# A transformer kernel on one core: two norm reductions placed later, an early strip split, halves in attention, and splits done one stage ahead

## The chip, the cores and the metric

The kernel runs on one core of one Trainium2 chip, in a single launch. The metric is device time in microseconds (us), the median of three runs. The engines are TensorE (PE, the matrix unit), VectorE (DVE), ScalarE (ACT), GpSimd (POOL) and SyncE (SP, which only issues transfers here).

## The reference

Two blocks run one behind the other on 512 tokens of width 1024 (256 context tokens beside them in the first block), all in float32:

```python
# first block, two layers
ax = modulate(rmsnorm(h, norm1_g[l]), mx[0], mx[1])
yx, yc = mixing_layer(ax @ w_in[l], ac @ w_in[l], ...)      # pooling, neighbourhood attention, retention
h = h + mx[2] * (yx @ w_out[l])                             # output projection
h = h + mx[5] * conv_ffn(modulate(rmsnorm(h, norm2_g[l]), mx[3], mx[4]), w_up[l], ..., w_down[l])
# conv_ffn: u = h @ w_up; a 3-tap convolution; (silu(a) * b) @ w_down, with 2816 hidden columns
# second block, one layer
h = rms(x, mix_norm_g); p = h @ w_in
a_out = mla(...)                                            # latent attention, 8 heads
h_out = hyena(...)                                          # long convolutions through DFTs
x = x + concat(rms(a_out), rms(h_out)) @ w_out
x = x + mem_xattn(rms(x), rms(mem), ...)                    # memory attention, 4 heads
x = x + hier_moe(rms(x), ...)                               # 32 experts
```

## The kernel before, in words

Activations lie transposed in SBUF: 8 tiles of 128 features by 512 or 768 columns (tokens, and the context's in the first layer). Weights come from HBM as 178 "strips" of up to 128x2048 float32, in the order in which they are used, into a ring of three slots.

**High and low parts.** TensorE takes float32 here only as a rounded form. So each operand is split in two: ScalarE writes the rounded value (`split_high`, L824), VectorE subtracts it from the value (`split_low`, L859), and three matmuls (high weight by low source, high by high, low by high) take the place of one. A strip's high part goes into one of two buffers that alternate, so the split of strip s waits until strip s-2 has been used up; its low part is written over the strip. Sources (the activation tiles) are split in the same way, each into a room of its own.

**`project` (L878 to L1028)** is one stage: it multiplies all sources by a list of strips. A unit is one output tile: it runs over all sources (`for j, tile in enumerate(u.tiles)`), six matmuls a source at 768 columns (three parts by two pieces) and three at 512. `split_order` (L908 to L923) is the order for both ScalarE and VectorE, written out by hand:

```python
if not ahead:
    split_strip(0)
following = max(1, ahead)
for k in range(tiles_ahead, len(sources)):
    if k == early and following < 2:
        split_strip(following)
        following += 1
    split_tile(k)
for i in range(len(units)):
    while following < total and (following < 2 or self.freed_at[first + following - 2] < ends[i]):
        split_strip(following)
        following += 1
    if deferred and i == 0:
        norm()
    take(i)
```

`take(i)` on VectorE evicts unit i from PSUM; on ScalarE it adds a bias or does what the stage hangs on it, once VectorE has taken unit i. `norm()` comes before `take(0)`. Strip 2 is split in turn i = 2 where strip 0 serves units 0 and 1, which is after `norm()`, `take(0)` and `take(1)`. `ahead` says that the first strip was split in the stage before, `tiles_ahead` how many sources were, and `early` ahead of which source strip 1 is split (if not given: behind all of them).

**Deferred norms.** The RMS norm in front of a projection is applied to its outputs. Beside the matmuls, ScalarE squares the tiles, VectorE adds the squares, TensorE sums them over partitions with a matmul by ones (`mean`, L437, or L533 in `PairNorm`), ScalarE takes the root, VectorE the reciprocal, and the eviction multiplies by it. TensorE does the summing matmul in `before(pe, 2)`, ahead of unit 2. `Deferred` serves the input projection of both layers (12 strips, two units each) and the up projection, `PairNorm` the second block's input projection (`second_projection`, 8 strips, two units each; its two sums and two roots make a longer chain).

**The stages around it.** A layer is input projection, pooling, neighbourhood attention, (context attention in layer 0), retention, output projection, up projection, down projection. In the down projection a unit needs two strips of 11 sources each, out of 22 sources. Layer 1's up projection splits the first 9 of these sources and the first strip ahead; layer 0's splits none. Retention splits the first strip of the output projection ahead, but no source. `attention` (L1030) runs over units of 128 queries (32 units in the latent attention, 16 in the memory attention): scores, maximum and scaling on VectorE (`top`, `normalise`), exponentials on ScalarE, transposes (L1123), a copy on ScalarE, products with the values at each head's end. Both of these attentions split the next stage's two first strips ahead: ScalarE in unit 4, VectorE in unit 5. No stage begins on any engine until all engines have left the one before.

## Time and profile before

| | |
|---|---|
| median of 3 runs | 2773.83 us (2773.24 to 2775.17) |
| the profiled execution: its own time | 2779.62 us |
| the profiled execution: span, first to last instruction | 2777.8 us |
| mean granted TensorE clock | 0.949 of full speed |
| TensorE busy | 2487.8 us (90% of the span), 14602 matmuls |
| VectorE busy | 1375.2 us (50%) |
| ScalarE busy | 868.5 us (31%) |
| GpSimd busy | 251.7 us (9%) |
| TensorE waiting, longest groups | 25.0, 24.9, 15.1, 13.8, 13.3 us |

The span is 1.8 us shorter than the execution's own time: that much lies around it. The profiled execution took 5.8 us more than the median of the runs. A wait is given with the engine and line of the instruction that ended it. A granted clock of 0.50 is TensorE at 1.2 GHz, 1.00 is 2.4 GHz.

### The profile page before, as it was taken

What the parts mean: (1) busy time and instruction counts of PE and PEld (TensorE: products, weight loads), DVE (VectorE), ACT (ScalarE), POOL (GpSimd) and SP (SyncE); (2) the same over time, 40 slices, a digit from 0 to 9 for tenths busy, and PEclk for the clock granted to TensorE, in tenths of its full rate; (3) what the DMA queues carried; (4) which work ended last, traced back from release to release, by engine and by line L of the source; (5) the groups of instructions that cost most, each with busy time, mean ns of one, the idle gap of its engine ahead of it and who ended that gap; (6) DMA issues with size and microseconds to landing.
All of it is one profiled execution on the core that took longest, in us unless ns stands there. A gap on an engine that the chain in (4) does not pass through costs nothing. (4 is left out here: it accounts for less than half of the span.)

```text
span 2777.8 us, 34833 instructions
## 1 busy us (share of the span) xinstructions
PE 2487.8 (90%) x14602; PEld 1933.5 (70%) x14602; DVE 1375.2 (50%) x2185; ACT 868.5 (31%) x1385; POOL 251.7 (9%) x183
## 2 busy tenths in 40 slices
PE   7997988999998998997889999998977889898976
PEld 5885657888887787995669998764733368573322
DVE  4324554566667214325647777347565645423213
ACT  3222433332324113223444334233424642311001
POOL 0002520000000000003500000000042020011112
PEclk9998989999999999997989999999988999988999
DMA  5114731111111112115612223320201013348997
GB/s 240 61 54 106 269 128 46 46 61 61 63 69 38 53 63 82 61 69 142 224 46 92 92 92 117 111 82 31 87 0 54 0 61 137 121 188 326 421 421 292
DMA packets 58555, 326.88 MB, mean 118 GB/s; under 512 B 8157, under 2 KB 14429, under 8 KB 26461
## 3 DMA queue, kind: packets, MB, share of 16 engines
q1 hardware_dynamic: 45358, 302.76, 29.4%
q0 software_dynamic: 5696, 12.59, 1.2%
q10 hardware_dynamic: 7344, 9.28, 1.0%
q8 instruction: 117, 1.92, 0.3%
q14 instruction: 40, 0.33, 0.0%
HBM read 317.26 MB, written 12.58 MB: 119 GB/s over the span
## 5 line engine op out<-in xcount | busy, mean ns | idle before, releaser
L953 PE MATMUL ps<-work_rounded,ring_rounded 128*128 128x512 f32 (+1 forms) x2016 | 537.0, 354 | 19.1 <-DVE work_rounded L397 10.6
L953 PE MATMUL ps<-xn_rounded,ring_rounded 128*128 128x512 f32 (+2 forms) x2304 | 541.8, 347 | 0.0
L2003 PE MATMUL ps<-xn_rounded,ring_rounded 128*128 128x258 f32 (+2 forms) x2816 | 535.1, 312 | 0.0
L2003 PEld LDWEIGHTS ps<-xn_rounded,ring_rounded 128*128 128x128 f32 x2816 | 414.6, 191 | 31.2
L953 PEld LDWEIGHTS ps<-xn_rounded,ring_rounded 128*128 128x128 f32 x2304 | 373.4, 191 | 57.6 <-issue 0.2
L953 PEld LDWEIGHTS ps<-work_rounded,ring_rounded 128*128 128x128 f32 x2016 | 336.5, 192 | 76.3 <-DVE work_rounded L397 11.8
L953 PE MATMUL ps<-big_rounded,ring_rounded 128*128 128x512 f32 (+1 forms) x1200 | 326.3, 364 | 45.0 <-DVE big_rounded L859 25.0
L859 DVE TENSOR_TENSOR ring_rounded<-ring,ring_rounded 128x2048 fp32r<-128x2048 f32 (+2 forms) x94 | 189.1, 2015 | 266.5 <-ACT ring_rounded L824 266.5
L2003 PE MATMUL ps<-work_rounded,ring_rounded 128*128 128x256 f32 (+1 forms) x1232 | 280.2, 309 | 9.0 <-PEq L784 4.8
L953 PEld LDWEIGHTS ps<-big_rounded,ring_rounded 128*128 128x128 f32 x1200 | 203.4, 196 | 84.8 <-DVE ring_rounded L859 21.4
L824 ACT ACTIVATE ring_rounded<-ring 128x2048 fp32r<-128x2048 f32 (+2 forms) x94 | 158.2, 1687 | 314.7 <-PE ps L953 298.3
L2003 PEld LDWEIGHTS ps<-work_rounded,ring_rounded 128*128 128x128 f32 x1232 | 191.9, 191 | 21.5 <-issue 10.6
L2052 DVE TENSOR_TENSOR ring_rounded<-ring,ring_rounded 128x1024 fp32r<-128x1024 f32 x84 | 103.0, 1226 | 171.4 <-ACT ring_rounded L2017 171.4
L2017 ACT ACTIVATE ring_rounded<-ring 128x1024 fp32r<-128x1024 f32 x84 | 89.0, 1060 | 205.8 <-PE ps L2003 205.8
L2022 ACT ACTIVATE work<-work,small 128x512 f32<-128x512 f32 (+1 forms) x132 | 81.5, 649 | 203.0 <-DVE work L2059 203.0
L1313 ACT ACTIVATE big<-big,small 128x512 f32<-128x512 f32 (+1 forms) x81 | 47.0, 624 | 254.0 <-DVE big L1309 154.0
L1303 DVE COPY small<-ps 128x2 f32<-128x2 f32 x46 | 7.3, 159 | 176.9 <-PE ps L953 176.6
L3320 PE MATMUL ps<-big,work 128*64 128x512 f32 x352 | 80.4, 604 | 15.1 <-DMA big<-in_experts 13.8
L1339 POOL MEMSET work<- 128x792 f32 x2 | 1.5, 758 | 1015.4 <-DMA work<-in_pool 1015.4
L2070 DVE SCALAR_TENSOR_TENSOR work<-work,vec 128x769 f32<-128x769 f32 (+1 forms) x88 | 78.0, 887 | 3.1
L2069 DVE SCALAR_TENSOR_TENSOR work<-work,vec 128x769 f32<-128x769 f32 (+1 forms) x88 | 78.0, 887 | 3.1
L3343 ACT ACTIVATE work<-ps,small 128x256 f32<-128x256 f32 x16 | 7.6, 476 | 221.3 <-PE ps L3320 221.3
(420 smaller groups left out, 3125.4 us busy)
## 6 DMA issues: line engine op xcount, KB each, us to landing
ring<-in_stream SPq DMA_DIRECT2D x141, 1024.0 KB, 4.8
big<-in_experts SPq DMA_DIRECT2D x44, 1024.0 KB, 26.0
ring<-in_stream SPq DMA_DIRECT2D x32, 704.0 KB, 4.0
ring<-in_experts SPq DMA_DIRECT2D x22, 1024.0 KB, 27.3
xn<-in_experts SPq DMA_DIRECT2D x15, 1024.0 KB, 28.4
work<-in_experts SPq DMA_DIRECT2D x15, 1024.0 KB, 28.7
big<-in_first_modulation SPq DMA_DIRECT2D x8, 1024.0 KB, 14.1
work<-in_bias ACTq DMA_DIRECT2D x24, 256.0 KB, 3.9
```

The source lines that it names most:

```text
L824: return act.activation(self.rounded(high), value, ACT.Copy)
L859: return dve.tensor_tensor(self.rounded(value), value, self.rounded(high).bitcast(F32), ALU.subtract)
L953: mm = pe.matmul(out[:, a - u.first:b - u.first], lhs, rhs, start=j == 0 and n == 0 and not u.onto, stop=j == terms - 1 and n == len(passe ...
L1313: act.activation(px[:, m, a:z], px[:, m, a:z], ACT.Identity, bias=bias[:, m, s:s + 1])
L2003: mm = pe.matmul(out[:, a:b], ws[:, k, :], x[k][:, a - base:b - base], start=k == 0 and n == 0, stop=k == KT - 1 and n == 2)
L2017: act.activation(high_w[c], half(i, c)[0], ACT.Copy).then_inc(strip_high.up(), 1)
L2022: ins = act.activation(u[:, i % 2, c, o:o + b - a], u[:, i % 2, c, o:o + b - a], ACT.Identity, bias=bias[:, i % 2, c, s:s + 1])
L2052: dve.tensor_tensor(low_part, value, high_w[c].bitcast(F32), ALU.subtract).then_inc(strip_low.up(), 1)
L2069: settle(dve, dve.scalar_tensor_tensor(out=cc, in0=uu[:, 0:n], scalar=cw(0, t), in1=cc, op0=ALU.mult, op1=ALU.add), vstep)
L2070: dve.scalar_tensor_tensor(out=cc, in0=uu[:, 2:2 + n], scalar=cw(2, t), in1=cc, op0=ALU.mult, op1=ALU.add).then_inc(convolved.up(), 1)
L3320: mm = pe.matmul(b.bank(2)[r, :], self.rows_t[:, k, r], self.gu[s][:, k, :], start=k == 0, stop=k == KT - 1)
L3343: act.activation(self.silu_t, b.bank(2)[:, 0:256], ACT.Silu, scale=b.slot_scale[:, 0, n:n + 1]).then_inc(self.silued, 1)
```

## The change

1. `PairNorm`: the two summing matmuls stand ahead of unit 4 and no longer ahead of unit 2.
2. `Deferred` in `project`: the summing matmul stands inside unit 2, after five of its eight sources, and no longer ahead of it.
3. `attention`: the two strips that are split ahead are split in four halves of 1024 columns, on ScalarE in units 4, 6, 8 and 10, on VectorE in units 5, 7, 9 and 11.
4. Down projections: strip 1 is split ahead of source 8 (layer 0) or 10 (layer 1) and no longer behind all sources.
5. Layer 0's up projection splits the down projection's first strip and first source at its end. Both retentions split the first source of the output projection.

```diff
 class PairNorm:  def before(self, pe, i):
-        if i == 2:
+        if i == 4:
             pe.wait_ge(b.sig("squares_added").sem, b.sig("squares_added").at(2 * KT - 2))
 project, tensor:
-                    if deferred:
+                    if deferred and not (i == 2 and type(deferred) is Deferred):
                         deferred.before(pe, i)
...
                         mine = j * len(u.need) // terms
+                        if i == 2 and j == 5 and type(deferred) is Deferred:
+                            deferred.before(pe, i)
 attention, vector:
+                def halves_low(part):
+                    for _, value, high in views[part // 2:part // 2 + 1]:
+                        r = slice(part % 2 * 1024, part % 2 * 1024 + value.shape[1] // 2)
+                        dve.wait_ge(strip_high.sem, strip_high.at(part + 1))
+                        self.split_low(dve, value[:, r], high[:, r])
...
-                    if u == 5:
-                        self.low_ahead(dve, views)
+                    if u in (5, 7, 9, 11):
+                        halves_low((u - 5) // 2)
 attention, scalar:
-                    if u == 4:
-                        self.high_ahead(act, views)
+                    if u in (4, 6, 8, 10):
+                        halves_high((u - 4) // 2)
 retention, scalar (behind root(0)):
+                act.wait_ge(weighed.sem, weighed.at(6))
+                for value, high in mixed:
+                    self.split_high(act, value, high).then_inc(next_high.up(), 1)
                 act.activation(self.small[:, 124:125], self.ones[:, 0:1], ACT.Ln)
                 square(2)
 retention, vector:
                 gate(2)
+                for n, (value, high) in enumerate(mixed):
+                    dve.wait_ge(next_high.sem, next_high.at(n + 1))
+                    self.split_low(dve, value, high)
                 normalise(1)
 ffn_up, scalar (layer 0 only):
+                    if (i, c) == (FT - 1, 1) and need_ctx:
+                        act.wait_ge(done.sem, done.at(2 * FT))
+                        strip_ahead(act)
                 silu(FT - 1)
+                if need_ctx:
+                    act.wait_ge(gated.sem, gated.at(len(runs)))
+                    self.split_high(act, *down_sources[0]).then_inc(next_high.up(), 1)
 ffn_up, vector (layer 0 only):
                 convolve(*halves_of[-1])
+                if need_ctx:
+                    strip_low_ahead(1)
                 gate(FT - 1)
+                if need_ctx:
+                    dve.wait_ge(next_high.sem, next_high.at(2))
+                    self.split_low(dve, *down_sources[0])
 down_sources (layer 0):
-            rooms, ahead = tiles_in(width, self.xn, self.work), 0
+            rooms, ahead = tiles_in(width, self.xn, self.work), 1
 ffn_down:
-        self.project(units, 2 * KT, finish, banks_each=2, sources=sources, tiles_ahead=tiles_ahead,
+        self.project(units, 2 * KT, finish, banks_each=2, sources=sources, tiles_ahead=tiles_ahead, early=10 if last else 8,
 layer: output_projection(...)
+                               tiles_ahead=1)
```

## Rows read from the trace of the kernel before

**Rows 1.** Waits of TensorE over the whole span: total, times, longest (us).
```profile
PE ps L953 <- DVE big_rounded L859: 25.0, 3, 12.1
PE ps L1123 <- DVE work L1156: 24.9, 21, 6.0
```

**Rows 2.** Timeline, second block's input projection, TensorE: start, length, idle before.
```profile
1920.23 1.98 PE L533 MATMUL ps<-xn,base 128*128 128x512 f32 x4 [2.30 <-DVE xn L547]
...
1937.35 0.79 PE L953 MATMUL ps<-work_rounded,ring_rounded 128*128 128x512 f32 x1 [4.02 <-DVE ring_rounded L859]
```

**Rows 3.** Timeline of the same stage, ScalarE and VectorE.
```profile
1933.06 1.91 ACT L824 ACTIVATE ring_rounded<-ring 128x2048 fp32r<-128x2048 f32 x1 [7.74 <-DVE big L2291]
...
1935.00 2.29 DVE L859 TENSOR_TENSOR ring_rounded<-ring,ring_rounded 128x2048 fp32r<-128x2048 f32 x1 [2.03 <-ACT ring_rounded L824]
```

**Rows 4.** Timeline, input projection of layer 0, TensorE and VectorE.
```profile
59.12 1.45 PE L437 MATMUL ps<-work,base 128*128 128x512 f32 x4
...
71.61 2.29 DVE L859 TENSOR_TENSOR ring_rounded<-ring,ring_rounded 128x2048 fp32r<-128x2048 f32 x1 [3.01 <-ACT ring_rounded L824]
...
77.36 0.51 PE L953 MATMUL ps<-work_rounded,ring_rounded 128*128 128x512 f32 x2
```

**Rows 5.** Timeline, input projection of layer 1, TensorE.
```profile
1109.81 2.93 PE L437 MATMUL ps<-work,base 128*128 128x512 f32 x4 [2.77 <-DVE work L412]
...
1125.14 0.47 PE L953 MATMUL ps<-work_rounded,ring_rounded 128*128 128x256 f32 x2 [0.72 <-DVE ring_rounded L859]
```

**Rows 6.** Timeline, end of layer 0's up projection and start of its down projection.
```profile
887.62 1.03 DVE L2077 TENSOR_TENSOR big<-work 128x512 f32<-128x512 f32 x2
889.01 1.38 ACT L824 ACTIVATE ring_rounded<-ring 128x1408 fp32r<-128x1408 f32 x1 [3.32 <-PEq L784]
...
891.96 7.04 DVE L859 TENSOR_TENSOR big_rounded<-big,xn_rounded 128x768 fp32r<-128x768 f32 x8
...
893.05 0.98 PE L953 MATMUL ps<-big_rounded,ring_rounded 128*128 128x512 f32 x2 [12.07 <-DVE big_rounded L859]
...
911.07 3.16 DVE L859 TENSOR_TENSOR ring_rounded<-ring,ring_rounded 128x1408 fp32r<-128x1408 f32 x2
912.74 1.01 PE L953 MATMUL ps<-big_rounded,ring_rounded 128*128 128x512 f32 x2 [5.70 <-DVE ring_rounded L859]
```

**Rows 7.** Timeline, start of layer 1's down projection, VectorE.
```profile
1733.05 1.62 DVE L859 TENSOR_TENSOR ring_rounded<-ring,ring_rounded 128x1408 fp32r<-128x1408 f32 x1
```

**Rows 8.** Timeline, retention's end and output projection's start, both layers.
```profile
418.57 0.84 ACT L1779 ACTIVATE big<-big 128x768 f32<-128x768 f32 x1 [0.51 <-DVE big L1870]
...
427.18 5.98 ACT L824 ACTIVATE work_rounded<-big 128x768 fp32r<-128x768 f32 x8 [1.56 <-PEq L784]
429.07 1.01 PE L953 MATMUL ps<-big_rounded,ring_rounded 128*128 128x512 f32 x2 [7.18 <-DVE big_rounded L859]
...
1409.34 4.27 ACT L824 ACTIVATE work_rounded<-big 128x512 fp32r<-128x512 f32 x8 [1.24 <-PEq L784]
1410.74 0.80 PE L953 MATMUL ps<-big_rounded,ring_rounded 128*128 128x512 f32 x1 [5.74 <-DVE big_rounded L859]
```

**Rows 9.** Attention's strip splits (timeline), and half-size splits (the page's groups).
```profile
2162.37 4.50 DVE L859 TENSOR_TENSOR ring_rounded<-ring,ring_rounded 128x2048 fp32r<-128x2048 f32 x2 [1.35 <-ACT ring_rounded L824]
...
2406.42 0.69 PE L1123 MATMUL ps<-base,work 128*128 128x128 f32 x2 [5.68 <-DVE work L1156]
...
L2052 DVE TENSOR_TENSOR ring_rounded<-ring,ring_rounded 128x1024 fp32r<-128x1024 f32 x84 | 103.0, 1226 | 171.4 <-ACT ring_rounded L2017 171.4
L2017 ACT ACTIVATE ring_rounded<-ring 128x1024 fp32r<-128x1024 f32 x84 | 89.0, 1060 | 205.8 <-PE ps L2003 205.8
```

**Rows 10.** Windows behind three waits: us, busy by engine, then the granted clock.
```profile
912.70:917.00 4.30, 4.26 (x13) 3.68 (x14) 1.53 (x1) 0.00 (x0) 0.00 (x0) 0.50 0.00 0
1109.80:1112.60 2.80, 2.79 (x5) 1.57 (x6) 0.00 (x0) 0.00 (x0) 0.00 (x0) 0.50 0.48 202
...
1937.30:1942.60 5.30, 5.25 (x13) 4.15 (x14) 3.27 (x3) 1.91 (x1) 0.00 (x0) 0.52 0.03 14
```

More of the change, by code:

```diff
@@ L1058, in attention @@
         views = self.split_ahead(ahead)
-        next_high = self.sig("next_high")
+        next_high, strip_high = self.sig("next_high"), self.sig("strip_high")
+        assert all(value.shape[1] == STRIP for _, value, _ in views)
         def pair_at(u, place):
@@ L1197, in exponentials, with halves_high @@
                                    accum_out=stat[:, 2, b:b + 1]).then_inc(exped.up(), 1)
+                def halves_high(part):
+                    for n, value, high in views[part // 2:part // 2 + 1]:
+                        r = slice(part % 2 * 1024, part % 2 * 1024 + value.shape[1] // 2)
+                        self.strip(act, n)
+                        self.split_high(act, value[:, r], high[:, r]).then_inc(strip_high.up(), 1)
                 def square_pair(p):
@@ L1654, in retention @@
         half = [slice(0, 64), slice(64, 128)]
+        next_high = self.sig("next_high")
+        mixed = [(px[:, MIXED[k], 0:qw], w[:, k * qw:(k + 1) * qw]) for k in range(1)]
         def update(c, d, p):
@@ L1979, in views @@
         def views():
-            return self.split_ahead(0 if need_ctx else 1)
+            return self.split_ahead(1)
         with self.stage() as block:
@@ L2023, in shift, with strip_ahead @@
                     ins.then_inc(shifted.up(), 1)
+                def strip_ahead(act):
+                    for number, value, room in views():
+                        self.split_high(act, self.strip(act, number), room).then_inc(next_high.up(), 1)
                 def silu(i):
@@ L2038, in _ @@
                         silu(i - 1)
-                    if c == 1 and 0 <= i - 2 < tiles_ahead:
+                    if c == 1 and 0 <= i - 2 < tiles_ahead and not need_ctx:
                         act.wait_ge(gated.sem, gated.at(len(runs) * (i - 1)))
                         self.split_high(act, *down_sources[i - 2]).then_inc(next_high.up(), 1)
-                    if (i, c) == (FT - 1, 0):
-                        for number, value, room in views():
-                            self.split_high(act, self.strip(act, number), room).then_inc(next_high.up(), 1)
+                    if (i, c) == (FT - 1, 0) and not need_ctx:
+                        strip_ahead(act)
+                    if (i, c) == (FT - 1, 1) and need_ctx:
+                        act.wait_ge(done.sem, done.at(2 * FT))
+                        strip_ahead(act)
                 silu(FT - 1)
+                if need_ctx:
+                    act.wait_ge(gated.sem, gated.at(len(runs)))
+                    self.split_high(act, *down_sources[0]).then_inc(next_high.up(), 1)
             @block.vector
@@ L2070, in convolve, with strip_low_ahead @@
                     dve.scalar_tensor_tensor(out=cc, in0=uu[:, 2:2 + n], scalar=cw(2, t), in1=cc, op0=ALU.mult, op1=ALU.add).then_inc(convolved.up(), 1)
+                def strip_low_ahead(count):
+                    for _, value, room in views():
+                        dve.wait_ge(next_high.sem, next_high.at(count))
+                        self.split_low(dve, value, room)
                 def gate(i):
@@ L2092, in _ @@
                         gate(i - 1)
[L2093 removed]
+                    if c == 1 and 0 <= i - 3 < tiles_ahead and not need_ctx:
                         dve.wait_ge(next_high.sem, next_high.at(i - 2))
                         self.split_low(dve, *down_sources[i - 3])
[L2096 to L2099 removed]
+                    if (i, c) == (FT - 1, 0) and not need_ctx:
+                        strip_low_ahead(tiles_ahead + 1)
                 convolve(*halves_of[-1])
+                if need_ctx:
+                    strip_low_ahead(1)
                 gate(FT - 1)
+                if need_ctx:
+                    dve.wait_ge(next_high.sem, next_high.at(2))
+                    self.split_low(dve, *down_sources[0])
     def down_sources(self, l, width):
         if l < DEPTH - 1:
[L2106 removed]
+            rooms, ahead = tiles_in(width, self.xn, self.work), 1
         else:
```

7 lines of the change are left out of this document (1 added, 6 removed).

## Prediction

> **What bounds the kernel now.** I read the cores' view first, then the page, then who made TensorE wait, then timelines around each place that the change touches. TensorE is busy for 90% of the span (the table above), so a place matters only by the time that TensorE stands still in it, and by the clock it has afterwards. The waits [rows 1] name two of the places: 25.0 us in three waits for a source's low part at a stage's start, and 24.9 us in 21 waits for attention's scaling, the longest 6.0 us. The others are short: 2.30 and 4.02 us in the second block's input projection [rows 2], 2.77 and 0.72 us in layer 1's input projection [rows 5], 12.07 and 5.70 us around layer 0's down projection [rows 6], 7.18 and 5.74 us ahead of the output projections [rows 8]. Behind such waits TensorE runs at 1.2 GHz for a while: over the whole 4.3 us behind the wait of 5.70, the whole 2.8 us behind that of 2.77, nearly the whole 5.3 us behind that of 4.02 [rows 10]. Half of that time is lost too. The sum is over places, one by one. Plus is slower.
>
> **1. `PairNorm` sums ahead of unit 4: +8.9.** Before, the sum waits 2.30 us for the squares and starts at 1920.23; TensorE then works through units 2 and 3, and waits 4.02 us for strip 2's low part until 1937.35 [rows 2]. What is that low part late for? Its high part on ScalarE was released by an eviction (L2291), and VectorE waited for that high part [rows 3]. In `split_order` strip 2 comes in turn 2, behind `norm()`, `take(0)` and `take(1)`, and `norm()` begins with the sum. So the chain is sum, two roots and reciprocals, two evictions, strip 2's high part, its low part: from 1920.23 to 1935.00 + 2.29 = 1937.29, or 17.06 us, all behind the summing matmul. And unit 4 needs strip 2 (two units a strip). After the change TensorE reaches unit 4 with nothing to wait for: 1937.35 - 4.02 - 2.30 - about 1.6 for the sum = 1929.4. There it does the sum, and then waits for the whole chain: 1929.4 + 17.06 = 1946.5, against 1937.35. That would be +9.1. The 2.30 us wait is gone, and the 4.02 us wait becomes about 15.4. A little may come off since the sum no longer starts behind a wait; I take +8.9. The clock is low behind either wait, so no difference is charged for it. From below: +8.0; from above +9.5, and another 1 if the low clock lasts longer.
>
> **2. `Deferred` sums inside unit 2, layer 0: +2.5.** Before, this sum waits for nothing and starts at 59.12; strip 2's low part is ready at 71.61 + 2.29 = 73.90, and TensorE reaches unit 4 at 77.36, 3.46 us later [rows 4]. So there is cover of 3.46 us. A source takes (77.36 - 59.12 - 1.1)/16 = 1.07 us here, the 1.1 being the sum itself. Five of them move the sum, and the chain to strip 2 with it, by 5.3 us, to 79.2. TensorE still comes at 77.36: it waits 1.9 us. The clock behind a wait this short: 0 to 1.2 us lost (the 2.8 us window at 0.50 behind a wait of 2.77 is the nearest row [rows 10]). I take 0.6.
>
> **The same, layer 1: +1.4.** The first reading is a gain of 2.77 us plus the slow sum behind it: the squares are ready at 1109.8, and TensorE, free from 1109.81 - 2.77 = 1107.0, gets to the sum after five sources at about 1110.7 with no wait (a source is 1.07 x 514/768 = 0.72 us, since these units are 514 columns wide). But unit 4 again starts on strip 2, with a wait of 0.72 us until 1125.14 [rows 5], behind the same chain. What matters is when the sum ends. Before: 1109.81 + 2.93 = 1112.74 at the low clock. After: 1110.7 + 1.45, the length of layer 0's sum [rows 4], = 1112.1. So unit 4 starts 0.6 us earlier, and the 2.77 us appear again as a wait of about 4.8 us ahead of unit 4. Behind it the clock is low where it was full before: 4.3 to 5.3 us at 1.2 GHz behind waits of 5.70 and 4.02 [rows 10] lose 2.0 to 2.7 us. I take 2.0. Bounds: -0.6 to +2.1.
>
> **3. Halves in attention: -0.4.** Before, the latent attention's VectorE stands 1.35 us for the high part and then works 4.50 us on two low parts [rows 9]; this is TensorE's wait of 6.0 us [rows 1]. Some 1.4 us more go in the slow clock behind it: 7.4. After, four pairs come one by one, 1.06 us on ScalarE and 1.23 us on VectorE [rows 9], 4.9 us of VectorE's time. VectorE's 5.85 us were all seen by TensorE, so its loop has hardly any idle time, and a pair costs 1.2 us where ScalarE's half is hidden (unit 8, beside the values' matmuls) and up to 2.3 where neither is. I take 1.9, 1.9, 1.2 and 1.6 = 6.6: a gain of 0.7. In the memory attention the wait of 5.68 [rows 9] shrinks to 2.5, but of the four pairs only the first and third have ScalarE's half hidden: -3.2 + 0.7 + 1.1 + 1.7 = +0.3. From -8 (the halves vanish in idle time) to +3 (2.3 for each of eight).
>
> Against this part speaks the Trainium skill, "VectorE: DVE Perf Modes", section "The TRN2 errata": each instruction reading SBUF pays a fixed latency, a large tile once and many small ones each time. Its float32 formula, (N+151)/0.96 ns, gives an estimate of 2291 ns for 2048 columns and 1224 for 1024, so 0.16 us for each of four splits, 0.6 in all. The trace agrees, with 1226 ns for 1024 [rows 9]. By the rule alone part 3 would be +0.6 instead of -0.4, since it doesn't see the waits.
>
> **4. and 5. Layer 0's down projection: -9.8.** Two pieces. (a) The start: before, VectorE ends the last gate at 887.62 + 1.03 = 888.65, the next stage begins at 889.01, and TensorE at 893.05, once ScalarE (1.38) and VectorE have split the strip and the first source [rows 6]. After, ScalarE does its two pieces behind its last bias, while VectorE convolves; VectorE puts the strip's low part (1.6) in front of the gate and the source's (0.88, as 7.04/8) behind it. Stage end 888.65 + 2.45 = 891.1, handover 0.36, TensorE at 891.45: -1.6. The last gate, delayed by 1.6, holds nobody but the stage's end. (b) Strip 1: before, it is split behind all 22 sources, from 911.07; TensorE, which needs it at source 11, waits 5.70 us, and then runs at 1.2 GHz for at least 4.3 us [rows 6, 10]: 5.70 + 2.5 = 8.2. After, it is split ahead of source 8: VectorE is past it 7 x 0.88 + 1.6 us behind the start of the sources, about 900, and source 11 is wanted at about 905. Sources then come each 0.88 us, TensorE takes 1.05 for one, so no other wait arises: tile 8 is ready at 900.9 and wanted at 901.8. That margin of 0.9 us is the thinnest cover. If the sources were late the gain would fall to about -5.
>
> **4., layer 1: 0.** Here nine sources are split ahead; strip 1's low part is ready at 1733.05 + 1.62 = 1734.67 [rows 7], and TensorE, at source 11 at 1735.1, has no wait there. Nothing to gain; sources 10 to 21 come 1.6 us later than before with more than 4 us of cover.
>
> **5., output projections: -2.5.** With its first source split ahead, TensorE starts with the stage, as ScalarE does: layer 0 at 427.18 and not 429.07, layer 1 at 1409.34 and not 1410.74 [rows 8]. Against this, ScalarE's copy stands in retention's last chain (square, logarithm, root). In layer 0 it takes 5.98/8 = 0.75, of which 0.51 was idle ahead of the square [rows 8]: -1.89 + 0.24 = -1.65. In layer 1 there is no such idle time: -1.40 + 4.27/8 = -0.87. VectorE's part lies in its wait for the root. Source 1's low part is ready 1.8 us into the stage, about as TensorE, still at 1.2 GHz, ends source 0. Bounds: -3.3 (copy hidden) to -1.
>
> **The sum.** 8.9 + 2.5 + 1.4 - 0.4 - 9.8 - 2.5 = +0.1. Against the profiled execution: 2777.8 + 0.1 of span, 2779.7 its own time. The median of the runs lies 5.8 lower than that execution: **2773.9 us**. Large terms of both signs cancel; this is the forecast, not absence of effect.
>
> **The rivals.**
>
> *The late sum is covered (faster).* If strip 2 of the second block's input projection did not hang on the norm, part 1 would be about -2 (its 2.30 wait gone), and the total 2773.9 - 11 = 2763. For it: TensorE's 2.30 us wait is real. Against it: ScalarE's high part was released by the eviction [rows 3]. 7%.
>
> *The halves hide (faster).* If each of the eight pairs fell into idle time, part 3 would be about -8: 2766. For it: two long waits [rows 1, 9]. Against it: VectorE's 1.35 + 4.50 = 5.85 us make up nearly all of TensorE's 6.0 [rows 1, 9], so nothing of them was hidden. From the point where a pair costs under 1.2 us on average the total goes below 2768. 12%.
>
> *The clock falls in attention (slower).* Before, there is one long wait in each attention; after, four of 1 to 2.5 us each. If the granted clock fell to 0.50 over the latent attention's units 5 to 12, some 12 us of matmuls would take twice as long in part: +6 to +7, so 2780. It decides where the clock is under 0.7 between the first and the last half. Against it: waits of 1 us between dense matmuls leave the clock at full. 9%.
>
> *The early strip starves the down projection (slower).* If sources 8 onwards came later than TensorE wants them, each wait would bring the low clock back, and part 4 would shrink to -2: 2782. 7%.
>
> *Nothing is moved.* The same time by another way, with all waits where they were: 2774. That can be told from my forecast only in the trace. 3%.
>
> **How the numbers follow.** My forecast has 62%, with 2769 to 2779 as its own range (the bounds of parts 2, 3 and 5 added in their roots, and 1 to 2 us for the clock behind six changed waits). 0.2%, about what a measurement of this kernel can tell from no change, is 5.5 us: below 2768.3 is faster, above 2779.4 slower. Faster: the first two rivals and a tail of the forecast, 0.20. Slower: the third and fourth and a tail, 0.17. The rest, 0.63, is the same. The range 2765 to 2781 leaves out the first rival and most of the fourth.
>
> **What would show it.** Right: TensorE's wait at L533 gone and one of about 15 us behind it for L859 in the second block's input projection; new waits of about 2 us (layer 0) and 5 us (layer 1) ahead of unit 4 of the input projections, none at L437; no wait inside unit 0 of layer 0's down projection; output projections that start with ScalarE. Wrong: that wait under 12 us, a clock under 0.7 in the latent attention's first half, or waits at sources 8 to 21.

## The result and the profile after

The changed kernel takes 2779.64 us (median of 16 executions, 2775.78 to 2789.01), the kernel before on the same chip 2775.43 us (16 executions, 2773.24 to 2780.5): a ratio of 1.0018, 95% interval 1.0011 to 1.0025, or +5.0 us (3.1 to 6.9). The forecast was +0.1 us and 2773.9, inside a range of 2765 to 2781. So "the same within 0.2%" came true, near its edge, and the sum was about 5 us short. In absolute time 2779.64 is 5.7 us above the forecast, just outside the forecast's own range of 2769 to 2779 and just past its border of 2779.4. Of these 5.7 us, 1.6 are not the change's: they are the kernel before, whose median is 2775.43 over 16 executions and was 2773.83 over the first three. The profiled execution has a span of 2780.2 us (before 2777.8) and a time of 2782.08.

Executions of the changed kernel are more spread than those of the one before: 13 of these 16 lie between 2775.8 and 2782.2, three at 2788 to 2789. That matters below. Two disturbed executions of the third group of experiments (6200 us of the kernel before, 3623 us of the changed one) are left out of all counts.

The mean granted clock of the profiled execution is 0.944 (before 0.949). Two of TensorE's waits over the whole span (total, times, longest) answer to [rows 1]:

```profile
PE ps L955 <- DVE ring_rounded L859: 24.2, 4, 15.1
...
PE ps L1126 <- DVE work L1159: 21.4, 22, 2.4
```

The 25.0 us for sources' low parts have left the top of the list; in their place are 24.2 us for strips' low parts, of which one wait is 15.1 us. Attention's longest wait went from 6.0 to 2.4 us, with 3.5 us less in total. Next is TensorE's timeline of the changed kernel at the seven places of the forecast: start, length, and in brackets the idle time before, with its releaser.

```profile
79.59 0.80 PE L955 MATMUL ps<-work_rounded,ring_rounded 128*128 128x512 f32 x2 [1.84 <-DVE ring_rounded L859]
...
429.13 0.98 PE L955 MATMUL ps<-big_rounded,ring_rounded 128*128 128x512 f32 x2 [5.33 <-PEq L784]
...
889.54 0.98 PE L955 MATMUL ps<-big_rounded,ring_rounded 128*128 128x512 f32 x2 [10.24 <-PEq L784]
...
1113.85 0.60 PE L955 MATMUL ps<-work_rounded,ring_rounded 128*128 128x256 f32 x2 [4.44 <-DVE ring_rounded L859]
...
1399.66 0.76 PE L955 MATMUL ps<-big_rounded,ring_rounded 128*128 128x512 f32 x1 [4.36 <-PEq L784]
...
1918.12 1.88 PE L533 MATMUL ps<-xn,base 128*128 128x512 f32 x4
...
1935.13 0.79 PE L955 MATMUL ps<-work_rounded,ring_rounded 128*128 128x512 f32 x1 [15.12 <-DVE ring_rounded L859]
```

Every wait is where the forecast put it, and nearly of its size: 1.84 us in layer 0's input projection (forecast 1.9), 4.44 in layer 1's (4.8), 15.12 in the second block's (15.4). The sum at L533 waits for nothing, where it had waited 2.30 us [rows 2]. From the sum's start to unit 4 it is 1935.13 - 1918.12 = 17.01 us; the same chain took 17.06 before.

To place time, the start of every tenth TensorE matmul is set against that of the same matmul before (both have 14602). The difference, called the offset below, is one execution against one:

| Place | Offset, us | Forecast |
|---|---|---|
| 1. `PairNorm` sum | -12.1 to -2.2: **+9.9** | +8.9 |
| 2. `Deferred`, layer 0 | **+3.5** | +2.5 |
| 2. `Deferred`, layer 1 | -10.5 to -9.8: **+0.7** | +1.4 |
| 3. latent attention | -2.2 to -2.6: **-0.3** | -0.7 |
| 3. memory attention | -2.6 to about -0.1: **+2.5** | +0.3 |
| 4./5. layer 0's down projection | -1.7 to -10.5: **-8.8** | -9.8 |
| 5. output projections | -1.4 and -1.7: **-3.1** | -2.5 |

These make +4.4. The other -2.0, down to the +2.4 of the spans, comes from stretches that the diff doesn't touch: -3.4 in layer 0's pooling and neighbourhood attention, -1.5 behind the wait of 2.79 us at the start of layer 0's up projection (last section), some +2.6 in the experts, and smaller steps elsewhere. Steps of that size in untouched code say how far one pair of profiles can be trusted; 14 profiles are kept in all, one of each run, and where they disagree on a place it is said below.

### The profile page after: what moved, and what is told of

Read it like the earlier page. It is cut to its first block and busy times, and to the rows that moved or that the text cites. A ratio compares the mean times of both kernels' runs of the same rounds, so it can differ in the third digit from the quotient of the medians.

```text
span 2780.2 us, 34841 instructions
## 1 busy us (share of the span) xinstructions
PE 2487.2 (89%) x14602; PEld 1933.8 (70%) x14602; DVE 1375.0 (49%) x2189; ACT 868.5 (31%) x1389; POOL 251.7 (9%) x183
## 5 line engine op out<-in xcount | busy, mean ns | idle before, releaser
L859 DVE TENSOR_TENSOR ring_rounded<-ring,ring_rounded 128x2048 fp32r<-128x2048 f32 (+3 forms) x98 | 190.0, 1939 | 260.6 <-ACT ring_rounded L824 260.4
L824 ACT ACTIVATE ring_rounded<-ring 128x2048 fp32r<-128x2048 f32 (+3 forms) x98 | 159.2, 1626 | 301.8 <-PE ps L955 288.5
L2027 PEld LDWEIGHTS ps<-work_rounded,ring_rounded 128*128 128x128 f32 x1232 | 191.6, 190 | 21.3 <-issue 10.6
## 6 DMA issues: line engine op xcount, KB each, us to landing
big<-in_experts SPq DMA_DIRECT2D x44, 1024.0 KB, 26.5
```

The source lines that it names most:

```text
L824: return act.activation(self.rounded(high), value, ACT.Copy)
L859: return dve.tensor_tensor(self.rounded(value), value, self.rounded(high).bitcast(F32), ALU.subtract)
L2027: mm = pe.matmul(out[:, a:b], ws[:, k, :], x[k][:, a - base:b - base], start=k == 0 and n == 0, stop=k == KT - 1 and n == 2)
```

## Experiments

Each experiment ran beside the kernel before. A ratio is to that kernel on the same chip and is not simply the quotient of the two medians (for e4 that quotient is 0.9946, the ratio 0.9957); us are worked out from the ratio with that kernel's median there (2777.14, 2777.75 and 2777.34 us in the three groups).

A "stretch" below is the time from one TensorE matmul to another, the same two in every profile.

### First group: one part undone at a time

**e1: part 1 undone.**

```diff
 # PairNorm.before
-        if i == 4:
+        if i == 2:
```

> The changed kernel with part 1 alone undone: the matrix for the sum of PairNorm stands ahead of unit 2 again. The forecast's sum charged that part +8.9 us, and the offset of TensorE between the two profiles rises by 9.9 us over this norm. So the forecast's theory: 9 to 10 us faster than the changed kernel (about 0.9965 of it), thus about 5 us faster than the kernel before; TensorE's wait of 15 us ahead of unit 4 is gone and waits of about 2 and 4 us stand again. Rival A (the late sum only looked costly in one profile): within 3 us of the changed kernel. Rival B (what is saved here is lost later, since the experts' tiles are bound by the transfers of their weights): the wait is gone and the end comes less than 4 us earlier.

2770.52 us, ratio 0.9989 (0.9975 to 1.0002). Against the changed kernel's 1.0018 that is 0.0029 or 8.0 us less (the two intervals make it 4 to 12). TensorE's timeline in this kernel:

```profile
1905.81 1.98 PE L533 MATMUL ps<-xn,base 128*128 128x512 f32 x4 [0.92 <-DVE xn L547]
...
1922.92 0.51 PE L955 MATMUL ps<-work_rounded,ring_rounded 128*128 128x512 f32 x1 [4.02 <-DVE ring_rounded L859]
```

The long wait is gone, the one of 4.02 us is back to the hundredth, and the profile's offset to the changed kernel goes from -2.3 to -12.9 us over the norm, 10.6 us. Both rivals fall: the late sum costs this much, and it isn't lost again in the experts (the spans differ by 13.5 us). Part of the 10.6 is the clock of single executions: the stretch of 215 matmuls around the sum takes 59.5 to 60.2 us in the five profiles with the sum ahead of unit 2 (the kernel before, e1, e4, e8, e9) and 67.8 to 70.1 in the six with the late sum (the changed kernel, e2, e3, e5, e10, e12), each of the six with the same wait of 15.12 us. So the late sum costs 7.6 to 10.6 us.

**e2: part 2 undone.** `deferred.before(pe, i)` is called ahead of every unit again, and the call at `i == 2 and j == 5` is taken out.

> The changed kernel with part 2 alone undone: in both layers the sum of squares of Deferred is called ahead of unit 2, not inside it. The forecast charged +2.5 us in layer 0 and +1.4 us in layer 1, the two profiles show about +3.5 and +0.7 us. So the forecast's theory: 3.5 to 4.5 us faster than the changed kernel (0.9985 of it). Rival (what layer 0 loses there it gains back in the neighbourhood part, where the changed kernel's offset fell by 3 to 4 us that nothing in the diff explains): within 1.5 us of the changed kernel, and the offset in the neighbourhood part doesn't fall.

2774.09 us, ratio 0.9995 (0.9984 to 1.0006): 0.0023 or 6.4 us less than the changed kernel (3 to 10). Layer 1's sum waits 2.8 us at L437 again and layer 0 has no wait ahead of unit 4. The profiles give 4.7 us between the spans. The mechanism holds; the size lies above the forecast's 3.9, within what can be told. Over all profiles the stretch around layer 0's sum takes 46.2 us wherever unit 4 doesn't wait, 48.3 in five of the profiles with the late sum, and 49.8 in the changed kernel's first one alone. So layer 0 costs 2.0 us as a rule, and the +3.5 of the table holds 1.5 us of clock. In layer 1 the same comparison gives 38.4 to 38.5 us in five profiles with the early sum (e2, e4, e7, e8, e11), 39.3 and 39.7 in the kernel before and e9, and 39.9 to 40.5 with the late sum.

**e3: part 3 undone.**

```diff
-                    if u in (5, 7, 9, 11):
-                        halves_low((u - 5) // 2)
+                    if u == 5:
+                        self.low_ahead(dve, views)
...
-                    if u in (4, 6, 8, 10):
-                        halves_high((u - 4) // 2)
+                    if u == 4:
+                        self.high_ahead(act, views)
```

> The changed kernel with part 3 alone undone: in the units of both attention stages the source is split ahead as whole strips again. The forecast's sum had -0.4 us for the halves (latent -0.7, memory +0.3), so by it this kernel is 0.4 us slower than the changed one, not to be told from it. Rival (what the two profiles show: latent -0.3, memory +2.5 us): about 2 us faster than the changed kernel (0.9992 of it), with the gain inside the memory attention alone. Rival of the other side (the halves hide the splits): 3 us or more slower.

2777.5 us, ratio 1.0007 (0.9996 to 1.0017): 0.0011 or 3.1 us less than the changed kernel (-0.4 to +6.6). The sign speaks for the first rival, though the interval holds 0, and the profiles show where. In the latent attention, these rows of TensorE begin with the same transpose ahead of the splits and end with the same one behind them; first the changed kernel, then e3:

```profile
2156.33 0.66 PE L1126 MATMUL ps<-base,work 128*128 128x128 f32 x4 [0.16 <-DVE work L1159]
2161.14 0.66 PE L1126 MATMUL ps<-base,work 128*128 128x128 f32 x4 [1.89 <-DVE work L1159]
...
2183.91 0.66 PE L1126 MATMUL ps<-base,work 128*128 128x128 f32 x4 [0.17 <-DVE work L1159]
```

```profile
2155.92 0.66 PE L1127 MATMUL ps<-base,work 128*128 128x128 f32 x4 [0.16 <-DVE work L1160]
2164.85 1.11 PE L1127 MATMUL ps<-base,work 128*128 128x128 f32 x4 [6.01 <-DVE work L1160]
...
2184.62 0.66 PE L1127 MATMUL ps<-base,work 128*128 128x128 f32 x4 [0.27 <-DVE work L1160]
```

27.58 us against 28.70. That looks like a gain of 1.1 us, but e3's profile is the odd one here: the same stretch takes 27.38 to 27.43 us in the six others with whole strips, and with halves 27.56 to 27.85 in five profiles and 26.5 in two (e10, e12). TensorE's idle time in it falls from 8.1 to about 5.6 us with halves, and its busy time rises from 19.3 us to 22 in the five and 20.8 in the two; the granted clock over it is 0.88 in the kernel before and 0.81 in the changed one. So here the halves do shorten the waits, by 2.5 us, and the clock takes all of it back in five executions and more than half of it in two. In the memory attention, the changed kernel and then e3:

```profile
2400.56 0.45 PE L1126 MATMUL ps<-base,work 128*128 128x128 f32 x2 [2.41 <-DVE work L1159]
2406.23 0.44 PE L1126 MATMUL ps<-base,work 128*128 128x128 f32 x2 [1.59 <-DVE work L1159]
2414.46 0.67 PE L1126 MATMUL ps<-base,work 128*128 128x128 f32 x2 [2.41 <-DVE work L1159]
2420.35 0.44 PE L1126 MATMUL ps<-base,work 128*128 128x128 f32 x2 [1.82 <-DVE work L1159]
...
2427.69 5.40 PE L1111 MATMUL ps<-work,big 128*128 128x512 f32 x8 [0.81 <-ACT work L1249]
```

```profile
2405.98 0.69 PE L1127 MATMUL ps<-base,work 128*128 128x128 f32 x2 [5.68 <-DVE work L1160]
2410.75 0.44 PE L1127 MATMUL ps<-base,work 128*128 128x128 f32 x2 [0.30 <-DVE work L1160]
2417.85 0.44 PE L1127 MATMUL ps<-base,work 128*128 128x128 f32 x2 [1.28 <-DVE work L1160]
2421.53 0.44 PE L1127 MATMUL ps<-base,work 128*128 128x128 f32 x2 [1.29 <-DVE work L1160]
...
2428.87 3.70 PE L1112 MATMUL ps<-work,big 128*128 128x512 f32 x8 [0.81 <-ACT work L1256]
```

The waits shown sum to 8.23 us with halves and 8.55 with whole strips: 0.3 less. But the same eight matmuls at the end take 5.40 instead of 3.70 us. The windows from the start of the first wait to the attention's end (us, busy by engine, granted clock), changed kernel and e3:

```profile
2398.15:2434.20 36.05, 24.30 (x69) 13.54 (x69) 20.89 (x52) 12.93 (x36) 0.00 (x0) 0.86 0.02 8
```

```profile
2400.30:2433.68 33.38, 21.32 (x69) 12.00 (x69) 20.76 (x50) 10.21 (x33) 0.00 (x0) 0.90 0.04 14
```

With halves the stretch is 2.7 us longer, TensorE's busy time grows by 3.0 us for the same 69 matmuls, and the granted clock is 0.86 instead of 0.90. So in the memory attention the halves turn one wait of 5.68 us into several of about 2, take next to nothing off the total, and pay the clock more often. The other profiles bear this out: up to the attention's end, from the last matmul ahead of the first wait, it is 33.7 to 33.8 us in all seven with whole strips, and with halves 36.0 to 36.4 in five, 34.3 in e10 and 39.1 in e2, with the granted clock of e2 at 0.78 over its stretch.

**e4: parts 1, 2 and 3 undone together.** What stays are parts 4 and 5.

> Parts 1, 2 and 3 undone together, so that of the change only the strip and source split in the up projection and the source split in the stages ahead of both output projections stay. The forecast's sum gives those parts -9.8 and -2.5 us: 12.3 us faster than the kernel before (0.9956 of it), some 12.4 us faster than the changed kernel by the terms, 16 us by the difference of the two medians. Rival (the part of layer 0's down projection is worth less than the profiles show, because an early start is given back in a wait for weights): less than 8 us faster than the kernel before. If the parts add up, e4 lies as far below the changed kernel as e1, e2 and e3 together, within 2 us.

2762.18 us, ratio 0.9957 (0.9942 to 0.9971): 11.9 us faster than the kernel before (8 to 16), where the forecast's terms say 12.3. The three parts together account for 1.0018 - 0.9957 = 0.0061, 16.9 us; singly they made 8.0 + 6.4 + 3.1 = 17.5. They add up.

### Second group: what makes the late sum dear

**e5: the changed kernel again.**

> The changed kernel once more, beside the kernels of this group, so that differences from it are not taken across chips. Expected: 4 to 6 us slower than the kernel before (ratio 1.0015 to 1.002). If the earlier figures of the changed kernel were a chip's own, it lies within 2 us of the kernel before.

2784.76 us, ratio 1.0029 (1.0012 to 1.0046). Six of the 12 executions lie between 2773.2 and 2780.5, the other six between 2789.0 and 2794.6 (these are called long below). The six lower ones have a median of 2778.1, 0.3 us above the kernel before; the six upper ones, at a mean granted clock of 0.940 to 0.943, make the whole difference. The ratio lies above the expected 1.0015 to 1.002, which its interval still holds.

**e6: strip 2 split between the squares and the wait for the sum**, in `Deferred` and `PairNorm`, on both engines; all else as in the changed kernel.

```diff
 # split_order
                 if deferred and i == 0:
-                    norm()
+                    norm(lambda: split_strip(2))
+                    following = 3
 # on_scalar: squares, then between(), then the root
 # on_vector: sums of squares, then
+        if between:
+            between()
         dve.wait_ge(b.sig("summed").sem, b.sig("summed").at(1))
```

> The changed kernel, with strip 2 of the three input projections that carry a norm split between the squares of the norm and the wait for its sum, not behind the norm and the evictions of units 0 and 1. My theory says that part 1 costs time only because unit 4's weights hang on the norm by that order, so that a later sum makes a later strip. By it the wait of 15.1 us ahead of unit 4 of the last input projection is gone, and with it the waits that parts 2 left (about 2 us in layer 0, 5 us in layer 1): 18 to 22 us faster than the changed kernel, some 14 to 16 us faster than the kernel before (0.9945). Rival A (unit 4 is held by the late norm itself, through the bank that it reuses or through the matrices of the sum): the wait of 15 us stays at another releaser, less than 5 us gained. Rival B (the split in the middle delays the root and so the evictions, and the wait moves to units 6 and 7): the wait ahead of unit 4 is gone and others of 3 us or more stand ahead of unit 6 or 7, 8 to 15 us gained.

2760.74 us, ratio 0.9946 (0.9931 to 0.9961): 15.0 us faster than the kernel before. Against the changed kernel beside it (e5) it is 24.0 us by the medians, 17.2 by the two spans, and 17.3 against the median of e5's six lower executions; none of e6's six is as long as e5's upper ones. In this kernel, VectorE:

```profile
1896.81 2.29 DVE L867 TENSOR_TENSOR ring_rounded<-ring,ring_rounded 128x2048 fp32r<-128x2048 f32 x1 [1.12 <-ACT ring_rounded L832]
1906.23 0.69 DVE L557 TENSOR_SCALAR work<-ps 128x512 f32<-128x512 f32 x1 [7.13 <-PE ps L539]
...
1920.33 2.29 DVE L867 TENSOR_TENSOR ring_rounded<-ring,ring_rounded 128x2048 fp32r<-128x2048 f32 x1 [2.19 <-ACT ring_rounded L832]
```

and TensorE's sum and one wait in that stage:

```profile
1904.32 1.88 PE L539 MATMUL ps<-xn,base 128*128 128x512 f32 x4
...
1922.77 0.77 PE L967 MATMUL ps<-work_rounded,ring_rounded 128*128 128x512 f32 x1 [5.47 <-DVE ring_rounded L867]
```

Strip 2 is now ready at 1899.1, before the sum, and neither unit 4 here nor unit 4 in the layers waits (the waits of 1.84 and 4.44 us are gone too). The wait of 15.12 us was therefore the split's place behind `norm()`, and not the norm itself: rival A falls. What is left is rival B in part: 5.47 us two units later, for strip 3, whose split still stands behind the evictions. The edit serves three stages. Against e5's profile the stretch around the sum is 2.0 us shorter in layer 0, 6.2 in layer 1 and 10.9 in the second block.

**e7: the same on top of e4** (sums ahead of unit 2, whole strips in attention).

> The kernel with parts 1, 2 and 3 undone, and strip 2 split between the squares and the wait for the sum. The sums stay ahead of unit 2, so their waits of about 2.4 us (the last input projection) and 2.8 us (layer 1) stay; only the wait of 4.0 us for strip 2 ahead of unit 4 of the last one can go, and small ones of the layers. Expected by my theory: 4 to 6 us faster than without it, thus 16 to 18 us faster than the kernel before (0.994). Rival (the order of the split is worth nothing, since unit 4 waits for the norm anyway): 12 us faster than the kernel before, as without it.

2759.58 us, ratio 0.9941 (0.9921 to 0.9961), 16.4 us faster than the kernel before; against e4's 0.9957 the gain of 4.4 us is inside the noise of the times, but the spans differ by 4.9 us (2758.6 and 2753.6) and the profile has the cause. TensorE in that stage, e4 and then e7:

```profile
1900.87 1.98 PE L533 MATMUL ps<-xn,base 128*128 128x512 f32 x4 [2.38 <-DVE xn L547]
...
1917.97 0.79 PE L953 MATMUL ps<-work_rounded,ring_rounded 128*128 128x512 f32 x1 [4.02 <-DVE ring_rounded L859]
```

```profile
1901.45 1.98 PE L539 MATMUL ps<-xn,base 128*128 128x512 f32 x4 [2.39 <-DVE xn L553]
```

One wait of 2.39 us, and none of 4.02. An early sum with an early strip 2 (2.39 us) is better than a late sum with it (5.47 us): the stretch around the sum is 53.6 us here (55.2 in e11) against 59.1 in e6 and 60.1 in e4.

**e8: the down projections alone**, e4 without the split ahead in the output projections.

> Of the change only the strip and the source split in the up projection, and the strip of the down projections split early; both output projections again start without a split source, and parts 1 to 3 are undone. The forecast's sum gives the down projections -9.8 us: 0.9965 of the kernel before; and the output projections -2.5 us, so this kernel is 2.5 us slower than the one with both. Rival (both output projections gave more, as the offsets of the profiles have it, some 4 us): 8 us faster than the kernel before and 4 us slower than the one with both. Rival (the early strip starves the down projection): slower than the kernel before, with waits for tiles 8 to 21.

2766.09 us, ratio 0.996 (0.9947 to 0.9973): 11.1 us faster than the kernel before (7 to 15; forecast 9.8). The early strip starves nothing: behind its start at 891.0 us TensorE has no wait above 0.3 us in layer 0's down projection up to 970 us. What the output projections add can't be read from e4 and e8: 0.8 us by the ratios, 3.9 by the medians, 8.1 by the spans.

### Third group: the output projections, and the long executions

**e9: the output projections alone**, on the kernel before.

```diff
+                act.wait_ge(weighed.sem, weighed.at(6))
+                for value, high in mixed:
+                    self.split_high(act, value, high).then_inc(next_high.up(), 1)
...
+                for n, (value, high) in enumerate(mixed):
+                    dve.wait_ge(next_high.sem, next_high.at(n + 1))
+                    self.split_low(dve, value, high)
...
+                               tiles_ahead=1)
```

> The kernel before with one part of the change alone: the first source of both output projections is split at the end of the retention. The forecast's sum gives it -2.5 us (0.9991). Rival (what the kernels with and without it showed, some 5 us): 0.998. Second question: of the executions of the changed kernel a share of about a quarter lies 10 to 15 us above the rest, at a granted clock of 0.940 to 0.943, and none of the 62 of the kernel before and of the 5 without this part does. If this part brings these, 2 to 5 of some 12 executions here lie 10 us or more above the others; if not, none.

2773.35 us, ratio 0.9983 (0.9974 to 0.9992): 4.7 us faster (2.2 to 7.2). A gain of its own, which the forecast's 2.5 is only just consistent with. Two of 11 executions lie 10 us above the lowest (2777.12 and 2777.52), but at a clock of 0.948 and at the end of an even spread, not apart.

**e10: the changed kernel without them.**

> The changed kernel without the split of the first source of the output projections. By the forecast's term it is 2.5 us slower than the changed kernel. If that part brings the long executions, none lies 10 us above the rest here and the median falls, though that of the common ones rises by 2.5 us; if another part brings them, a quarter or more is still long.

2778.76 us, ratio 1.001 (0.9998 to 1.0022). Two of 12 executions are long (2788.2 and 2790.6). So the output projections don't bring them alone. That this kernel isn't 2.5 us slower than the changed one (0.0008 less, interval of the difference 4 us to either side) says nothing against e9, since the changed kernel carries more long executions.

**e11: e7 without the output projections.**

> The kernel with parts 1, 2 and 3 undone and strip 2 split between the squares and the wait for the sum, here without the split in the output projections too. By the terms it is 2.5 us slower than with it, 14 us faster than the kernel before (0.995). If the split in the output projections brings long executions, this one has none, and its mean is no worse than with it.

2757.59 us, ratio 0.9939 (0.9923 to 0.9956), 16.9 us faster than the kernel before, not to be told from e7. One of six executions is long (2767.7, the lowest 2754.7), three of six in e7. e7 and e11 are the fastest versions.

**e12: the changed kernel a third time.**

> The changed kernel again, beside the two without a part of it: common executions 0 to 4 us above the kernel before, and 2 to 5 of 12 of them 10 us above these. Should the profiled one be of the long kind, its record of the clock tells in which stage the time lies; by the forecast's rival of the clock that is the attention of the latents.

Ratio 1.0021 (1.0004 to 1.0038). Six executions at 2770.1 to 2780.3 (median 2776.3, 1.0 us below the kernel before) and five at 2786.7 to 2793.4, with clocks of 0.941 to 0.943. The profiled one, with a span of 2776.1, was again not of the long kind.

## Why the forecast was right, and where its sum was short

**Large terms that cancel: right.** e4 and e8 show the gains (-11.9 and -11.1 us against -12.3 and -9.8), e1, e2 and e3 the losses. The class "same" is a difference of two effects of 12 and 17 us, not absence of effect. That so little was left in the sum is in part luck: the terms' errors have both signs, and the long executions, below, stood in no term.

**1. The late sum (+8.9; offset +9.9, e1 8.0, all profiles 7.6 to 10.6).** Right in mechanism, place and size. The chain took 17.01 us as it had. TensorE reached the sum 0.9 us later than worked out: at 1918.12 + 12.13, the offset there, = 1930.3 on the old profile's clock, against 1929.4. The rival "the late sum is covered" is refuted, and e6 shows the condition that it named: once strip 2 doesn't hang on the norm, the long wait is gone.

**2. Inside unit 2 (+3.9; offsets +4.2, e2 6.4).** The waits came as stated. The clock behind them was not the same from execution to execution. These are windows of 3.4 us behind the same wait in layer 0 (us, busy by engine, granted clock), first the changed kernel's profile, then that of e5, which is the same kernel:

```profile
79.60:83.00 3.40, 3.40 (x11) 2.91 (x12) 1.84 (x5) 2.52 (x5) 0.00 (x0) 0.53 0.60 255
```

```profile
79.60:83.00 3.40, 3.40 (x21) 3.01 (x20) 1.54 (x4) 2.83 (x5) 0.00 (x0) 1.00 0.58 243
```

1.84 us of idle time ahead (1.83 in e5), eleven matmuls at 1.2 GHz in one execution and 21 at 2.4 GHz in the other. The forecast took 0.6 us for it; beside the idle time TensorE's busy time grows by 0.2 us in five profiles and by 1.7 in one. In layer 1 the forecast took from one profile that the sum runs slowly, for 2.93 us [rows 5]; in e4 and e2, with the sum in the same place behind the same wait of 2.79 us, these matmuls take 2.12 and 2.16 us, and the later wait of 0.72 us isn't there (the row is e4's):

```profile
1095.95 2.12 PE L437 MATMUL ps<-work,base 128*128 128x512 f32 x4 [2.79 <-DVE work L412]
```

Against those profiles the late sum costs 1.4 to 2.1 us in layer 1, against the kernel before's 0.6 to 1.2.

**3. Halves (-0.4; latent -0.3, memory +2.5, e3 +3.1).** This is the term that was mis-sized, near the edge of its bounds (-8 to +3). Its working has a slip of 0.1 us (7.4 - 6.6 is 0.8, not 0.7), which changes nothing. In the latent attention it took a gain of 0.7; the profiles show 0.1 to 0.5 us lost in five and 0.9 gained in two, since it charged the clock behind the old wait (1.4 us) and nothing behind the new ones. In the memory attention the forecast put -3.2 + 0.7 + 1.1 + 1.7 = +0.3, a sum of waits alone, and took from the rows that short waits leave the clock at full. The balance of waits was about right (-0.3), but behind the new waits of 2.41, 1.59, 2.41 and 1.82 us the clock fell three times (these three windows, from the changed kernel's profile):

```profile
2400.50:2403.00 2.50, 2.44 (x9) 1.96 (x10) 1.16 (x6) 1.95 (x5) 0.00 (x0) 0.57 0.00 0
...
2415.00:2418.00 3.00, 3.00 (x10) 2.33 (x10) 1.44 (x4) 2.83 (x7) 0.00 (x0) 0.51 0.02 5
...
2427.00:2430.00 3.00, 2.31 (x4) 1.00 (x5) 1.17 (x2) 0.63 (x2) 0.00 (x0) 0.70 0.00 0
```

That makes +3.0 us of busy time (windows of e3 above). It is the rival "the clock falls in attention", in both attentions and milder: 0.81 over the latent stretch and 0.86 over the memory attention's, not under 0.7. "The halves hide" is refuted.

**4. and 5. The down projection (-9.8; offset -8.8, e8 -11.1).** Right. VectorE of the changed kernel, which answers to [rows 6]:

```profile
885.75 1.62 DVE L859 TENSOR_TENSOR ring_rounded<-ring,ring_rounded 128x1408 fp32r<-128x1408 f32 x1
887.29 1.02 DVE L2115 TENSOR_TENSOR big<-work 128x512 f32<-128x512 f32 x2
888.23 0.95 DVE L859 TENSOR_TENSOR big_rounded<-big,xn_rounded 128x768 fp32r<-128x768 f32 x1
890.39 6.17 DVE L859 TENSOR_TENSOR big_rounded<-big,xn_rounded 128x768 fp32r<-128x768 f32 x7 [1.22 <-ACT xn_rounded L824]
896.48 1.62 DVE L859 TENSOR_TENSOR ring_rounded<-ring,ring_rounded 128x1408 fp32r<-128x1408 f32 x1
898.02 7.90 DVE L859 TENSOR_TENSOR big_rounded<-big,work_rounded 128x768 fp32r<-128x768 f32 x9
```

The strip's low part lies ahead of the last gate, the source's behind it, and TensorE starts with the stage (889.54, and ScalarE at 889.52). Strip 1 is ready at 898.1, and no wait follows in unit 0: the 5.70 us and the low clock behind them are gone. The thin cover of 0.9 us held, and "the early strip starves the down projection" is refuted. At the stage's start 1.8 us were gained (forecast 1.6).

**5. Output projections (-2.5; offset -3.1, e9 -4.7).** Right in kind: TensorE starts with ScalarE, which in the changed kernel reads:

```profile
429.10 3.05 ACT L824 ACTIVATE work_rounded<-big 128x768 fp32r<-128x768 f32 x4 [1.56 <-PEq L784]
...
1399.63 2.71 ACT L824 ACTIVATE work_rounded<-big 128x512 fp32r<-128x512 f32 x5 [1.23 <-PEq L784]
```

TensorE's starts are 429.13 and 1399.66. In e9 TensorE's idle time around the two starts is 1.74 and 0.88 us less than before, which is what the term held (1.65 and 0.87). The measured time is some 2 us more than the term; that the clock makes the difference (last section) is not shown.

**What no term held: the long executions.** Of the changed kernel's 39 executions in three groups (16, 12 and 11), 14 lie at 2786.7 to 2794.6, at clocks of 0.940 to 0.943. Of the 90 of the kernel before, none lies above 2782.2, and of the 74 whose clock is given none is under 0.945. The other 25 of the changed kernel have medians 3.4, 0.3 and -1.0 us from the kernel before's, and a common mean 1.5 us above it, where all 39 are 5.9 above; the forecast's sum was +0.1. So over the three groups most of the excess is this share of long executions. In the measured result itself, with 3 long of 16, it is the smaller part: the mean is 5.3 us above the kernel before's with them and 3.5 without. Why the three groups differ (3 of 16, 6 of 12, 5 of 11) is not known; e5 and e12 ran on two different chips. With one part undone long executions are rarer, 8 of 46 together (3 of 12 in e1, 2 of 11 in e2, 1 of 11 in e3, 2 of 12 in e10, of which four in all have a clock of 0.943 or less), but no single one of these kernels shows it beyond chance, and the changed kernel never ran on the chip of e1, e2 and e3. If it holds, e1, e2 and e3 each take credit for some of it, and their differences overstate the parts. Which stage holds the 10 to 13 us stays open: none of the profiled executions was of the long kind. That it is the clock behind the waits is argued from their mean clock, not shown.

## What to carry to other kernels

Before a reduction is moved later, follow what is queued behind its result in the other engines' written order: here a weight split that needed nothing from the norm stood behind it, and unhooking it in three stages took 17 us off the changed kernel's span (e6 against e5). In the second block's stage alone, unhooking it (59.1 us for the stretch around the sum) and moving the sum back (59.5) are worth the same, against 67.8 to 70.1 with neither, and both together give 53.6. To cut one long operation into pieces helps only where the pieces fall into idle time and the clock holds: in one attention here the total of the waits hardly changed, in the other it fell by 2.5 us, and in both the clock behind more waits took the gain back or more. Undo each part of a bundle by itself: this one held a gain of 12 us (e4) under losses of 17.

## What the runs showed of the hardware that was not expected

The granted clock behind one and the same wait differs from execution to execution. The start of layer 0's up projection has 2.79 us of idle time in the kernel before and in e9, and no edit is near it. TensorE in each, and the windows of 3.4 us behind it:

```profile
501.60 0.69 PE L2003 MATMUL ps<-work_rounded,ring_rounded 128*128 128x512 f32 x2 [2.79 <-PEq L784]
502.09 1.49 PE L2003 MATMUL ps<-xn_rounded,ring_rounded 128*128 128x512 f32 x4
...
501.60:505.00 3.40, 3.40 (x11) 2.96 (x12) 3.37 (x8) 3.17 (x5) 2.64 (x1) 0.55 0.42 176
```

```profile
498.64 0.59 PE L2012 MATMUL ps<-work_rounded,ring_rounded 128*128 128x512 f32 x2 [2.79 <-PEq L784]
499.07 0.86 PE L2012 MATMUL ps<-xn_rounded,ring_rounded 128*128 128x512 f32 x4
...
498.64:502.04 3.40, 3.40 (x19) 3.01 (x20) 3.36 (x8) 3.17 (x5) 2.64 (x1) 1.00 0.37 154
```

The same four matmuls take 1.49 us at 1.2 GHz in one and 0.86 at 2.4 GHz in the other. Each place with such a wait is worth 0 or about 1.5 us in one profile, and with several of them two profiles of one kernel differ by 3.8 us (2780.2 and 2776.4). An effect of one or two microseconds can't be read from one pair of profiles; it takes the waits themselves, which repeat to a few hundredths (15.12, 4.02, 2.79, 1.84), and medians of many executions.
